# A hybrid decoder layer with 32 experts on one core: an own order for the last pair of experts, and the branch for further pairs behind the output's stores

## The reference, cut to what matters

```python
def layer(x, c, ssm0, conv0, lp):
    ...
    x = x + gt_m * mix
    h = rmsnorm(x, lp['g_ffn']) * (1.0 + sc_f) + sh_f
    x = x + gt_f * moe(h, lp)          # top 4 of 32 experts for each token
    ...
    # an expert: g = min(x Wg + bg, 7), u = clip(x Wu + bu, -7, 7)
    #            y = (g * sigmoid(1.702 g) * (u + 1)) Wd + bd, times the token's weight
...
y_prompt = rmsnorm(yp, g_final)
y_sample = rmsnorm(ys, g_final)
```

## Time and profile before

| | |
|---|---|
| median of 3 runs | 1263.0 us (1262.57 to 1268.4) |
| the profiled execution's own time | 1262.95 us |
| its span, first to last instruction | 1260.7 us |
| PE busy | 1172.0 us (93%) |
| DVE busy | 307.8 us (24%) |
| ACT busy | 149.1 us (12%) |
| HBM read | 447.99 MB, 358 GB/s over the span |
| chain that ended last | PE 68%, DMA 25%, DVE 3%, ACT 2%, issue 2% |

### The profile page before, as it was taken

The page is one execution under the profiler, slowest core; times in us unless marked ns, Lnnn a source line. Parts: engine busy times, 40 slices in busy tenths (PEclk is TensorE's granted clock), DMA queues, the critical chain, the costliest instruction groups (busy, mean ns, idle before and its releaser), DMA issues.

```text
span 1260.7 us, 15492 instructions
## 1 busy us (share of the span) xinstructions
PE 1172.0 (93%) x6459; PEld 547.3 (43%) x6460; DVE 307.8 (24%) x668; ACT 149.1 (12%) x249; POOL 36.0 (3%) x44
## 2 busy tenths in 40 slices
PE   5899988959999999999999999999999999999993
PEld 2663556644535334242435353534434353425352
DVE  2231454250402122121212120212122121213024
ACT  1332222030101010010000000101000010000001
POOL 1010223000000000000000000000000000000000
PEclk8899986979999999999999999999999999999997
DMA  9435556654899999999999999999999999999931
GB/s 387 187 142 195 201 220 260 267 201 201 350 429 427 427 427 426 427 427 427 427 427 427 428 428 428 428 429 428 429 428 429 428 429 427 430 426 429 425 162 44
DMA packets 36341, 452.69 MB, mean 359 GB/s; under 512 B 3904, under 2 KB 6080, under 8 KB 6592
## 3 DMA queue, kind: packets, MB, share of 16 engines
q1 hardware_dynamic: 35968, 449.31, 84.9%
q0 software_dynamic: 320, 2.60, 0.5%
HBM read 447.99 MB, written 3.91 MB: 358 GB/s over the span
## 4 chain that ended last, share of the span: by engine, by line
PE 68%; DMA 25%; DVE 3%; ACT 2%; issue 2%; SPq 0%; DVEq 0%; ACTq 0%
PE ps L553 67%; DMA arena<-in_w_exp 23%; DMA arena<-in_w_front 2%; ACT arena L1149 2%; DVE arena L1205 1%; PE ps L907 1%; DMA arena<-in_xT 0%; SPq L484 0%; PE ps L791 0%; DVE arena L1664 0%; ACT arena L1195 0%; DVE arena L1412 0%; DVE arena L1211 0%; DVE arena L1409 0%; DVE arena L1662 0%
## 5 line engine op out<-in xcount | busy, mean ns | idle before, releaser
L553 PE MATMUL ps<-arena 128*64 128x512 f32 (+9 forms) x6214 | 1141.8, 529 | 75.7 <-DVE arena L1205 24.2
L553 PEld LDWEIGHTS ps<-arena 128*64 128x64 f32 (+4 forms) x6214 | 518.0, 150 | 690.5 <-issue 606.5
L1149 ACT ACTIVATE arena<-ps 128x1024 f32<-128x1024 f32 x49 | 48.4, 1021 | 556.1 <-PE ps L553 556.1
L1205 DVE TENSOR_TENSOR arena<-arena 128x1024 f32<-128x1024 f32 (+12 forms) x89 | 73.9, 854 | 78.2 <-ACT arena L1077 32.5
L1205 DVE TENSOR_TENSOR arena<-arena,ps 128x320 f32<-128x320 f32 (+2 forms) x132 | 65.1, 494 | 96.6 <-PE ps L553 90.9
L1519 DVE TENSOR_SCALAR arena<-ps 128x1024 f32<-128x1024 f32 x16 | 19.6, 1224 | 282.4 <-PE ps L553 282.4
L1523 DVE TENSOR_SCALAR arena<-ps 128x1024 f32<-128x1024 f32 x16 | 19.6, 1225 | 202.3 <-PE ps L553 202.3
L1157 ACT ACTIVATE arena<-arena 128x1024 f32<-128x1024 f32 x16 | 16.9, 1057 | 260.2 <-DVE arena L1519 260.2
L1512 DVE COPY arena<-arena 128x64 f32 (+3 forms) x32 | 5.0, 193 | 126.8 <-PE ps L553 126.8
L1505 DVE TENSOR_SCALAR arena<-arena 128x64 f32<-128x64 f32 (+3 forms) x96 | 22.9, 305 | 0.0
L1205 DVE TENSOR_TENSOR arena<-ps,arena 128x64 f32<-128x64 f32 (+10 forms) x37 | 12.2, 351 | 37.7 <-PE ps L553 31.1
(11 more groups left out here) (134 smaller groups left out, 159.7 us busy)
## 6 DMA issues: line engine op xcount, KB each, us to landing
arena<-in_w_exp SPq DMA_DIRECT2D x192, 2048.0 KB, 23.1
arena<-in_w_front SPq DMA_DIRECT2D x38, 1024.0 KB, 7.8
arena<-in_s0T SPq DMA_DIRECT2D x1, 2048.0 KB, 9.3
out_ssmsT<-arena POOLq DMA_DIRECT2D x1, 2048.0 KB, 6.6
arena<-in_xT SPq DMA_DIRECT2D x1, 1280.0 KB, 6.0
out_yT<-arena SPq DMA_DIRECT2D x4, 320.0 KB, 2.3
arena<-in_vec SPq DMA_DIRECT2D x1, 898.0 KB, 13.6
arena<-in_con SPq DMA_DIRECT2D x1, 624.0 KB, 7.0
```

Source lines behind the costliest of these rows:

```text
L553: return pe.matmul(o, l, r, start=start, stop=stop, skip_group_check=True)
L1149: A(moe[name].rearrange("p (a b) -> p a b", a=2), ps[:, bank:bank + 2, :], ACT.Copy).then_inc(done, 1)
L1205: return V.tensor_tensor(o, a, b, op)
```

## The change

The last pair, q = 15, gets functions of its own (`last_pair`, `last_copies`, `activate_last`, `add_last`), and the final normalisation another form (`final_sums`, `squares`, `final_norm`):

- No further pair's tokens are gathered in the last pair; `select_further(0)` and the gather move into the branch for further pairs.
- `combine(14)` and `turn_sel(15)` stand between the gate and the up product.
- VectorE adds `acc`, times the gate, to `xT` while the up product runs.
- The up and the down product end half by half of their 512 columns (`half_done`). Clip, transposes and copies of the activation, and the copy of the output, go in halves; the second four transposes stand inside the down product (`mid`).
- The last combine uses the 8 banks; VectorE adds its blocks, times the gate, from PSUM to `xT` (`add_last`).
- Squares go to a free ring slot, `y_sq`. They are summed in 8 matmuls of 32 rows in four places side by side, scaled, and summed again in one matmul; ScalarE's root reads that from PSUM and adds epsilon as a bias.
- The branch for further pairs stands behind the output's stores. If it is entered, the normalisation and the stores are done again.

```diff
-def further_pairs(engine, there, body):
+def further_pairs(engine, there, begin, body, again):
     with engine.If(there(engine, 0) == 1):
+        begin()
         body(0)
-    with engine.If(there(engine, 1) == 1):
-        with engine.Fori(1, MORE_PAIRS) as i:
-            with engine.If(there(engine, i) == 1):
-                body(i)
+        with engine.If(there(engine, 1) == 1):
+            with engine.Fori(1, MORE_PAIRS) as i:
+                with engine.If(there(engine, i) == 1):
+                    body(i)
+        again()
...
+        spare = [(HELD + PER * (LAST % UNROLL) + PER // 3 + i) % RING for i in range(2)]
+        y_sq = view(ring_at + spare[0] * LOAD, [KC, T])
+        y_fin = view(ring_at + spare[1] * LOAD, [KC, T])
...
+            def store_y(r):
+                for q in range(0, KC, 2):
+                    sp.wait_ge(yfin, r * KC + q + 2)
+                    sp.dma_start(out["yT"].rearrange("(c p) t -> p c t", p=P)[:, q:q + 2], y_fin[:, q:q + 2]).then_inc(st_y, 16)
...
+            store_y(0)
             sp.wait_ge(more_ready, 1)
-            further_pairs(sp, there, more_loads)
-            for q in range(0, KC, 2):
...
+            further_pairs(sp, there, stored, more_loads, store_again)
+            stored()
             sp.wait_ge(st_conv, 16)
...
+                    order = [(kk, half) for kk in range(CHUNKS) for half in range(2)]
+                    if half_done is not None and p == KC // CHUNKS - 1:
+                        order = [(kk, half) for half in range(2) for kk in range(CHUNKS)]
+                    for kk, half in order:
+                        if mid is not None and (p, kk, half) == (0, CHUNKS - 2, 0):
+                            mid()
+                        for c, s in tiles:
+                            last = mm(ps[c, bank + half, :], rows[:, CHUNKS * p + kk, c], w[s][:, kk, half * AW:(half + 1) * AW],
+                                      False, CHUNKS * p + kk == KC - 1)
+                            if kk == CHUNKS - 1 and half == 1 and c.stop in (wa, P):
+                                last.then_inc(exp_used, 1)
+                        if half_done is not None and (p, kk, half) == (KC // CHUNKS - 1, CHUNKS - 1, 0):
+                            last.then_inc(half_done, 1)
...
+            def last_pair(slots, loads):
+                q, third = LAST, PER // 3
+                pe.wait_ge(x_ready, q + 1)
+                pe.wait_ge(pick_ready, q + 1)
+                product(0, 0, X, loads[0:third], slots[0:third])
+                combine(q - 1)
+                turn_sel(q)
+                pe.wait_ge(comb_added, q * KC)
+                product(1, 2, X, loads[third:2 * third], slots[third:2 * third], half_done=up_half)
+                def turn_half(h):
+                    if h == 0:
+                        pe.wait_ge(act_half, 1)
+                    else:
+                        pe.wait_ge(act_ready, q + 1)
+                    for k in range(4 * h, 4 * h + 4):
+                        last = pe.transpose(ps[:, h, (k % 4) * P:(k % 4 + 1) * P], A[:, k, :], cn("ident"))
+                    last.then_inc(a_tr if h == 0 else a_tr_half, 1)
+                turn_half(0)
+                pe.wait_ge(actT_half, 1)
+                pe.wait_ge(y_ready, q)
+                product(2, 4, A, loads[2 * third:], slots[2 * third:], half_done=down_half, mid=lambda: turn_half(1),
+                        between=lambda: pe.wait_ge(actT_ready, q + 1))
+                pe.wait_ge(selT_ready, q + 1)
+                for m in range(KC):
+                    if m == 0:
+                        pe.wait_ge(y_half, 1)
+                    if m == KC // 2:
+                        pe.wait_ge(y_ready, q + 1)
+                    mm(ps[:, m, 0:T], moe["y"][:, m * P:(m + 1) * P], moe["selT"]).then_inc(comb_mm, 1)
+            def final_sums(r):
+                for q in range(2):
+                    pe.wait_ge(f_sq, 2 * r + q + 1)
+                    for g in range(4):
+                        last = mm(ps[32 * g:32 * g + 32, 0, 0:T], cn("ones")[:, 0:32], y_sq[:, 4 * q + g, :], q == 0, q == 1)
+                last.then_inc(f_sums, 1)
+                pe.wait_ge(part_ready, r + 1)
+                mm(ps[:, 1, 0:T], cn("ones"), rstd).then_inc(mean_mm, 1)
...
-            combine(PAIRS - 1)
+            final_sums(0)
...
+            def last_copies():
+                q = LAST
+                copy_sel(q)
+                for h in range(2):
+                    if h == 0:
+                        act.wait_ge(a_tr, q + 1)
+                    else:
+                        act.wait_ge(a_tr_half, 1)
+                    A(moe["g"][:, h * AW:(h + 1) * AW], ps[:, h, :], ACT.Copy).then_inc(actT_half if h == 0 else actT_ready, 1)
+                act.wait_ge(down_half, 1)
+                A(moe["y"][:, 0:AW], ps[:, 4, :], ACT.Copy).then_inc(y_half, 1)
+                act.wait_ge(exp_used, q * PER + PER)
+                A(moe["y"][:, AW:D], ps[:, 5, :], ACT.Copy).then_inc(y_ready, 1)
...
+            def squares(r):
+                for q in (0, 4):
+                    if r:
+                        act.wait_ge(more_added, 1)
+                    for m in range(q, q + 4):
+                        act.wait_ge(x2_ready, m + 1)
+                        A(y_sq[:, m, 0:TP], xT[:, m, 0:TP], ACT.Square)
+                    act.wait_ge(xs2_ready, q // 4 + 1)
+                    A(y_sq[:, q:q + 4, TP:T], xT[:, q:q + 4, TP:T], ACT.Square).then_inc(f_sq, 1)
+                act.wait_ge(eps_set, 1)
+                act.wait_ge(mean_mm, r + 1)
+                A(rstd, ps[:, 1, 0:T], ACT.Sqrt, bias=eps).then_inc(root_done, 1)
+            squares(0)
...
+            V.memset(eps, EPS).then_inc(eps_set, 1)
...
+            def activate_last():
+                q, g, s = LAST, moe["g"], moe["s"]
+                dve.wait_ge(exp_used, q * PER + PER // 3)
+                V.tensor_scalar(halves("g"), blocks(0), LIMIT, None, ALU.min).then_inc(g_ready, 1)
+                add_up(q - 1)
+                dve.wait_ge(sig_ready, q + 1)
+                step(tt(g, g, s, ALU.mult))
+                dve.wait_ge(comb_added, q * KC)
+                gated = Steps(dve, fold_steps)
+                for m in range(KC):
+                    prompt_chunk(m, acc[:, m, 0:TP])
+                gated(tt(by_seq(acc), by_seq(acc), wide(ada[:, GT_F, :, 1:9], 3, SL), ALU.mult))
+                gated(tt(by_seq(xT), by_seq(xT), by_seq(acc), ALU.add))
+                for h in range(2):
+                    gh, sh = g[:, h * AW:(h + 1) * AW], s[:, h * AW:(h + 1) * AW]
+                    if h == 0:
+                        dve.wait_ge(up_half, 1)
+                    else:
+                        dve.wait_ge(exp_used, q * PER + 2 * PER // 3)
+                    gated(V.tensor_scalar(sh, ps[:, 2 + h, :], LIMIT, -LIMIT, ALU.min, ALU.max))
+                    V.scalar_tensor_tensor(gh, sh, 1.0, gh, ALU.add, ALU.mult).then_inc(act_half if h == 0 else act_ready, 1)
+            def prompt_chunk(m, src):
+                return V.scalar_tensor_tensor(xT[:, m, 0:TP], src, ada[:, GT_F, m, 0:1], xT[:, m, 0:TP], ALU.mult, ALU.add)
+            def add_last():
+                for q in (0, 4):
+                    for m in range(q, q + 4):
+                        dve.wait_ge(comb_mm, LAST * KC + m + 1)
+                        prompt_chunk(m, ps[:, m, 0:TP]).then_inc(x2_ready, 1)
+                    held = acc[:, q:q + 4, TP:T].rearrange("p c (b j) -> p c b j", b=NSEQ)
+                    tt(held, ps[:, q:q + 4, TP:T].rearrange("p c (b j) -> p c b j", b=NSEQ),
+                       wide(ada[:, GT_F, q:q + 4, 1:9], 3, SL), ALU.mult).then_inc(comb_added, 4)
+                    dve.wait_ge(comb_added, LAST * KC + q + 4)
+                    tt(xT[:, q:q + 4, TP:T], xT[:, q:q + 4, TP:T], acc[:, q:q + 4, TP:T], ALU.add).then_inc(xs2_ready, 1)
+            def final_norm(r):
+                dve.wait_ge(f_sums, r + 1)
+                V.tensor_scalar(rstd, ps[:, 0, 0:T], 1.0 / (32 * D), None, ALU.mult).then_inc(part_ready, 1)
+                dve.wait_ge(root_done, r + 1)
+                V.reciprocal(rstd, rstd).then_inc(rstd_ready, 1)
+                dve.wait_ge(rstd_ready, r + 1)
+                for m in range(KC):
+                    V.scalar_tensor_tensor(y_fin[:, m, :], xT[:, m, :], vc("g_final")[:, m:m + 1], rstd, ALU.mult,
+                                           ALU.mult).then_inc(yfin, 1)
...
+                    if last:
+                        activate_last()
+                        continue
...
-            add_up(PAIRS - 1)
-            start = start + PAIRS * OWN + 2
+            add_last()
+            final_norm(0)
...
-            step(prompt_chunk(0))
-            prompt_chunk(1)
-            xs_seq, acc_seq = by_seq(xT), by_seq(acc)
-            step(tt(acc_seq, acc_seq, wide(ada[:, GT_F, :, 1:9], 3, SL), ALU.mult))
-            tt(xs_seq, xs_seq, acc_seq, ALU.add).then_inc(f_sq_in, 1)
```

(17 more changed lines are left out.)

89 lines of the change are left out of this document (42 added, 47 removed).

## The result

The changed kernel takes 1243.9 us (median of 4 runs, 1240.99 to 1248.16), the kernel before beside it 1263.1 us (1262.57 to 1268.4): ratio 0.984, 95% interval 0.981 to 0.987. The profiled execution took 1241.51 us, its span 1239.3 us, 21.4 us less than before.

A forecast was written before the change was run, and what follows sets the result against it. PE and DMA were both taken as full until the last weights land, then only the chain of engine waits matters. Savings 8.4 + 1.1 + 11.1 - 0.8 = 19.8 us, from 1262.95 to 1243.1 us; range 1239.5 to 1247.0.

The forecast's parts named there:

- From the gate read to the down product: From VectorE's read of the last pair's gate product to the end of the down product: saves 8.4 us.
- The last combine and the way to the mean: Behind the down product: last combine runs at once, saves 1.1 us; from combine to mean saves 11.1 us.
- the way to "slower": Rival: TensorE's pauses for VectorE's adds inside the combine bring its clock to 1.2 GHz, which stays: 1278 us; chance 2%.
- TensorE's branches: In the old kernel's tail, TensorE's two branches delay its sums: about 3.6 us of the tail.
- The root: From mean to reciprocal: the root's table load now waits for the mean, 1.9 us instead of 1.1; costs 0.8 us.
- The end: From reciprocal through eight products and stores to the end: unchanged at 8.7 us, nothing taken for branches.
- the rival's 3.9 us for SyncE: Rival: SyncE's branch behind the output stores takes TensorE's 3.9 us, exposed at the end: 2.5 us more, 1245.6 us; chance 18%.

The follow-up runs named there:

- late combine: Changed kernel with the combine of pair 14 and VectorE's adds moved back behind the up product: 3.55 us more than the changed kernel, ratio 0.986 to the kernel before.
- quarter unit: Changed kernel loading only 512 KB of the last 2 MB weight unit: 0.63 us less than the changed kernel, ratio 0.981 to the kernel before.
- undone halves: Changed kernel with up product, activation and down product of the last pair waited for as whole tiles: 6.4 us more, ratio 0.991 to the kernel before.
- detour by `acc`: Changed kernel with the last combine's blocks added to `acc` first, then folded into the residual: 5.0 us more, ratio 0.987 to the kernel before.
- early epsilon: Changed kernel with ScalarE's wait for epsilon moved to its start, so the root's table load carries no wait: 1.32 us less, median 1243.5 us, ratio 0.983.
- one round of sums: Changed kernel with epsilon waited for early and squares summed at once by full-width matmuls, scaled in the root: 58.00 us from last gate product's read to end, ratio 0.984.

## Why the prediction was right, and where not

**From the gate read to the down product** (8.4 forecast, 8.2 measured). The adds ended 5.2 us behind the gate read (5.5 forecast), the up product 20.2 (20.5), the down product started at 21.5 (21.6), and the last unit, 30.30 us after its issue (30.1 in the earlier trace rows), was the wait in its middle: 0.72 for 0.8 to 0.9. The late combine and the quarter unit show both waits to be what the step said. That the old wait for weights (2.71 us) and the lower clock behind it (8.78 us against some 7) had cost nearly as much as the moved combine was right as well: the up product ends 20.2 us behind the gate read; before, VectorE read its end at 19.8.

**The last combine and the way to the mean** (1.1 + 11.1 forecast, 12.8 measured). Blocks at 0.41 to 0.53 us, sums 0.75 and scale 0.49 came as costed. VectorE was done with its second half 6.0 us behind the down product's end instead of 6.8, so 0.8 us sooner. From the last square to the mean it took 2.2 us instead of some 2.0: I had taken 0.57 us for the last matmul from a row of eight that follow each other, and alone it took 0.81. The undone halves and the detour by `acc` show the direction, and one term I had too small: pauses of 3 us on TensorE cost themselves and, in these two kernels, 3.3 and 1.2 us more by the clock behind them. I had costed such a pause for the way to "slower", not as a part of what the halves save; the total was right because the changed kernel has no such pause.

**TensorE's branches** were costed at about 3.6 us. Taking all engines' branches out gave 5.8, of which some 4.6 are TensorE's, by an estimate from the rows (3.4 of gap and 1.2 of slower sums). In the sum this didn't show, since I went by the end of the mean. With all its branches gone, the changed kernel gains 0.3 us.

**The root** (0.8 forecast, 0.8 measured). The table load took 1.28 us and the next operation followed 1.29 us after its start. The drain of about 1.38 us that the Trainium skill charges ("ScalarE: Activation LUTs", What ACT_TABLE_LOAD costs) isn't there: the early epsilon won 1.32 us, the load and nothing more. (By that rule the sum would have come to 1243.1 + 1.38 = 1244.5 us, not to the 1244.3 of the prediction.)

**The end** (0 forecast, 0.8 measured) is the step that failed. "I take nothing for the branches" was right for what the branches occupy on their engines, 50 to 63 ns, and the rival's 3.9 us for SyncE didn't come. But I had bounded a branch by its time on its own engine. Behind the jump comes an instruction packet, it falls between the stores', and all four landings went from 2.3 to 3.1 us. Without that branch the packet is gone and the end is 8.70 us as before; how one packet comes to delay all four is argued, not shown. The Trainium skill ("Runtime: NRT & Kernel Launch", Instruction fetch mechanics) has the fetch, and I had read it only for what the jumping engine waits.

So a sum of 19.8 met 19.4 this closely with some luck, by misses that partly cancel: 0.6 us too little in the middle, 0.8 and 0.2 too much at the end and in front. The profiled execution's 1241.5 us lies 1.6 under the forecast only because it began its last pair 2.0 us early; the median of 1243.9 is 0.8 over it.

## What to carry to other kernels

In a tail where engines wait for each other, cut what they hand over into halves, and look how long TensorE stands still: here a stop of 2.95 us with one of 0.78 close behind it cost another 3 at the lower clock, one of 2.65 in another kernel nothing, and stops of 1.34 and 0.61 nothing in the changed kernel but 0.6 and 0.3 in two of its versions. Where the clock falls can't be told from the length of one stop. Leave a jump over much code where neither its engine nor a transfer that ends the kernel is in a hurry; its price may be paid in another queue. To judge a microsecond, compare from an event behind the scatter, not by the median of whole runs.

## What the runs showed that I had not expected

- A jump over the code of further pairs takes TensorE 3.3 to 4.3 us, ScalarE, VectorE and SyncE 0.05 to 0.06 us.
- With one instruction packet beside the stores (8 or 16 KB, 0.7 or 0.9 us long) their landing went from 2.4 to 3.1 us. With the late combine the packet took only 0.4 us, and they still landed after 3.1, so the delay isn't simply the packet's length.
- In the kernel with one round of sums the prompt's columns and the samples' columns were accumulated in one PSUM bank. The samples' first matmul, with its start flag, came in the middle of the prompt's eight, and the prompt's sum then lacked its first four blocks. The output for the prompt was off by a relative 0.416; half of the sum missing gives √2 − 1 = 0.414. The Trainium skill ("PSUM — Partial Sum Buffer", The four PSUM rules) says as much: a matmul that starts an accumulation marks all columns of its bank, in the rows that it writes, as not yet written, so that the next one there overwrites. The missing blocks agree with it.
